# Output projection as seven half-block products per 256 tokens, with row additions on GpSimd and the variance on ScalarE

## What is computed

```python
h    = x * (1 + scale(c)) + shift(c)
proj = h @ w_in + b_in            # q, k, v, z_attn, u_x, g_b, g_c, z_conv, g_A, g_B
y_A  = (dilated_window_attention(q, k, v) * silu(z_attn)) @ w_proj_attn
y_B  = (g_b * conv3(g_c * u_x) * silu(z_conv)) @ w_proj_conv
m    = sigmoid(g_A) * y_A + sigmoid(g_B) * y_B
out  = LayerNorm(alpha * x + gate(c) * (m @ w_out + b_out)) * ln_g + ln_b
```

## Time and profile before

| | |
|---|---|
| median of 3 runs | 1869.77 us (1869.06 to 1870.61) |
| the profiled execution's own time | 1868.47 us |
| its span | 1866.7 us |
| PE / VectorE / ScalarE / GpSimd busy | 99% / 65% / 45% / 10% |
| granted TensorE clock, mean | 0.999 of full |

### The profile page before, as it was taken

How to read it: one execution, slowest core, us unless ns; L and a number is a source line. 1 busy time by engine, 2 the same in 40 slices (tenths; PEclk the granted TensorE clock), 3 DMA queues, 4 the chain that set the end, 5 groups by cost and what they waited for, 6 DMA issues and landing times.

```text
span 1866.7 us, 24546 instructions
## 1 busy us (share of the span) xinstructions
PE 1849.8 (99%) x8879; PEld 1508.0 (81%) x8879; DVE 1214.1 (65%) x2086; ACT 840.7 (45%) x1493; POOL 183.0 (10%) x305
## 2 busy tenths in 40 slices
PE   8999999999999999999999999999999999999998
PEld 7788888888888888878878888888888888888886
DVE  8755744456666666675686766666657576646776
ACT  5644633445545555666674545555454310012221
POOL 0223011100000000111210000000111100000000
PEclk9999999999999999999999999999999999999999
DMA  9866523332322222455853222222354988784442
GB/s 372 296 234 242 200 111 113 98 128 72 111 88 95 86 95 82 153 190 180 296 212 101 94 80 91 82 88 87 113 176 135 287 238 225 219 276 135 147 136 101
DMA packets 156648, 292.38 MB, mean 157 GB/s; under 512 B 35344, under 2 KB 87312, under 8 KB 152816
## 3 DMA queue, kind: packets, MB, share of 16 engines
q1 hardware_dynamic: 131056, 202.87, 33.9%
q0 software_dynamic: 25184, 87.35, 12.7%
q10 hardware_dynamic: 288, 0.59, 0.1%
HBM read 202.37 MB, written 88.38 MB: 156 GB/s over the span
## 4 chain that ended last, share of the span: by engine, by line
PE 95%; DVE 2%; ACT 1%; DMA 1%; issue 1%; ACTq 0%; POOL 0%; DVEq 0%
PE acc L1120 22%; PE acc L1125 21%; PE acc L1128 21%; PE acc L1329 3%; PE acc L1278 3%; PE acc L1282 3%; PE acc L1321 3%; PE acc L1325 3%; PE acc L1274 3%; PE score L1185 2%; PE xb L1218 2%; PE acc L1136 1%; PE xb L1201 1%; PE pt_o L1201 1%; DMA vt_d<-room 1%
## 5 line engine op out<-in xcount | busy, mean ns | idle before, releaser
L1120 PE MATMUL acc<-t_hi,w_hi 128*128 128x512 f32 x1848 | 509.2, 397 | 3.0 <-DVE room L1625 1.8
L1125 PE MATMUL acc<-t_lo,w_hi 128*128 128x512 f32 x1848 | 495.0, 390 | 0.0
L1128 PE MATMUL acc<-t_hi,w_lo 128*128 128x512 f32 x1848 | 494.9, 390 | 0.0
L1125 PEld LDWEIGHTS acc<-t_lo,w_hi 128*128 128x128 f32 x1848 | 346.9, 188 | 74.1
L1128 PEld LDWEIGHTS acc<-t_hi,w_lo 128*128 128x128 f32 x1848 | 346.9, 188 | 73.8
L1120 PEld LDWEIGHTS acc<-t_hi,w_hi 128*128 128x128 f32 x1848 | 337.1, 188 | 82.2 <-issue 13.1
L1625 DVE TENSOR_TENSOR room<-acc,part 128x512 f32<-128x512 f32 x198 | 136.8, 691 | 219.7 <-PE acc L1128 213.9
L1421 ACT ACTIVATE part<-acc,cols 128x512 f32<-128x512 f32 x198 | 136.8, 691 | 209.8 <-PE acc L1128 209.4
L1625 DVE TENSOR_TENSOR room<-room 128x512 f32<-128x512 f32 (+3 forms) x223 | 176.5, 795 | 73.8 <-ACT room L1451 30.7
L1625 DVE TENSOR_TENSOR w_lo<-w_raw,w_hi 128x512 fp32r<-128x512 f32 x272 | 183.7, 687 | 40.8 <-ACT w_hi L1404 39.2
L1404 ACT CAST w_hi<-w_raw 128x512 fp32r<-128x512 f32 x264 | 162.8, 617 | 90.2 <-PE acc L1128 87.6
(11 more groups left out here) (224 smaller groups left out, 2067.8 us busy)
## 6 DMA issues: line engine op xcount, KB each, us to landing
w_raw<-in_w_tiles SPq DMA_DIRECT2D x132, 512.0 KB, 4.5
gate_d<-room POOLq DMA_DIRECT2D x64, 256.0 KB, 3.8
w_raw<-gate_d SPq DMA_DIRECT2D x32, 512.0 KB, 5.6
qk_d<-room POOLq DMA_DIRECT2D x24, 512.0 KB, 5.1
room<-qk_d SPq DMA_DIRECT2D x74, 128.0 KB, 3.6
t_raw<-tr_d SPq DMA_DIRECT2D x8, 1024.0 KB, 7.1
conv_d<-room POOLq DMA_DIRECT2D x16, 512.0 KB, 3.0
mix_d<-w_raw POOLq DMA_DIRECT2D x32, 256.0 KB, 5.6
```

What stands on the lines that cost most here:

```text
L1120: nc.tensor.matmul(to, w_hi[:, s, k], t_hi[:, p, k], start=(first and k == 0), stop=False, skip_group_check=True)
L1125: nc.tensor.matmul(to, w_hi[:, s, k], t_lo[:, p, k], start=False, stop=False, skip_group_check=True)
L1128: mm = nc.tensor.matmul(to, w_lo[:, s, k], t_hi[:, p, k], start=False, stop=(last and k == KH - 1), skip_group_check=True)
```

## The change

- The output projection becomes 8 more groups (`NO`) of the ring's scheme, 256 tokens each. The tiles of m take the part of the ring's weights (`load_m` into `w_raw`, then `combine`, `round_w`, `split_w`), the output weights the part of the stationary token blocks: seven 128x2048 blocks, four of them sums. PE runs `product(n)` for n from `NS` = 476 to `NALL` - 1 = 531.
- The four sums of the weights are made in mid-kernel, in four steps of a 1024 KB load, four subtractions of 128x512 on VectorE (`sum_wq`) and a 1024 KB store to `to_d` from GpSimd's queue.
- The seven weight blocks are loaded (`load_to`), rounded and split one by one as the merge gives their room free: blocks 0 to 3 during the last 8 units, blocks 4, 5 and 6 when all of `mc_done` (32) is reached, that is behind the last matmul of the merge.
- The merge's last 8 units use other buffers (`mg_last`), whose reload waits for the store of the tile three units earlier.
- LayerNorm: ScalarE scales x (`scale_x`), GpSimd adds the bias row (`residual`), VectorE adds the products onto it (`take_y`, four of seven with a running sum), ScalarE squares and sums for the variance and takes the root (`deviation`), VectorE subtracts the mean and multiplies by g (`center`), ScalarE divides (`scale_row`), GpSimd adds b and issues the store (`shift_row`). Only the last tile keeps `bn_stats` and halves.

```diff
+NO = NTT // 2
+NALL = NS + NO * NP
...
+            s = (n - NS) % RING
+            return t[1][:, RING - 1] if s == KH else t[0][:, 1, s].rearrange("p (k n) -> p k n", n=P)
...
+                def load_to(p):
+                    sp.wait_ge(mc_done, M0 + (0, 2, 4, 6, 8, 8, 8)[p])
...
+                        sp.wait_ge(t_hi_done, 3 * NP + T_MORE + p - 3)
+                    sp.dma_start(to_raw(p), src).then_inc(t_in[p % 4], 16)
...
+                    if tt in (2, 3, 4):
+                        wait_m_last()
...
+                load_to(4)
+                load_to(5)
+                load_to(6)
+                sp.wait_ge(gb_ready, 1)
...
+                for to, src in ((g_bc, ln_g), (b_bc, ln_b)):
+                    sp.dma_start(to, src.broadcast_to([P, D])).then_inc(bc_in, 16)
+                for tt in range(2, NX):
+                    load_x(tt)
+                for h in range(2, NO):
+                    load_m(h)
+                    for tt in (2 * h, 2 * h + 1):
+                        if tt >= NX:
+                            load_x(tt)
...
+                def residual(tt):
+                    pool.wait_ge(x_scaled, tt + 1)
+                    nc.gpsimd.tensor_tensor(xs[tt % NX], xs[tt % NX], gb, ALU.add).then_inc(r_ready, 1)
+                def shift_row(tt):
+                    pool.wait_ge(normed, tt + 1)
+                    nc.gpsimd.tensor_tensor(xs[tt % NX], xs[tt % NX], b_bc, ALU.add).then_inc(affine, 1)
+                    pool.wait_ge(affine, tt + 1)
+                    pool.dma_start(out2[tt * P:(tt + 1) * P, :], xs[tt % NX]).then_inc(outs[tt % 4], 16)
...
+                for tt in range(4):
+                    residual(tt)
+                pool.wait_ge(bc_in, 64)
+                for h in range(NO):
+                    shift_row(2 * h)
+                    if h < NO - 1:
+                        shift_row(2 * h + 1)
+                    for tt in (2 * h + 4, 2 * h + 5):
+                        if tt < NTT:
+                            residual(tt)
...
-                for tt in range(NTT):
-                    r = tt % 2
-                    pe.wait_ge(m_hi_done, tt + 1)
...
-                        for k in range(KT):
-                            if tt == 0 and half == 0 and k % 2 == 0:
-                                pe.wait_ge(wo_hi_done, k // 2 + 1)
-                            nc.tensor.matmul(to, m_h[:, k], wo_hi[:, k, w], start=(k == 0), stop=False)
...
+                for n in range(NS, NALL):
+                    product(n)
...
+                    act.wait_ge(nmu_ready, tt + 1)
+                    nc.scalar.activation(squares, xs[tt % NX], ACT.Square, bias=nmu[:, r:r + 1],
+                                         accum_out=ssq[:, r:r + 1]).then_inc(squared, 1)
+                    act.wait_ge(squared, tt + 1)
+                    nc.scalar.activation(std[:, r:r + 1], ssq[:, r:r + 1], ACT.Sqrt, bias=eps[:, 0:1],
+                                         scale=1.0 / D).then_inc(std_ready, 1)
...
+                def scale_x(tt):
+                    act.wait_ge(x_in[tt % 4], 16 * (tt // 4 + 1))
+                    nc.scalar.activation(xs[tt % NX], xs[tt % NX], ACT.Identity, bias=0.0, scale=ALPHA).then_inc(x_scaled, 1)
+                def scale_row(tt):
+                    r = tt % 2
+                    act.wait_ge(centered, tt + 1)
+                    nc.scalar.activation(xs[tt % NX], xs[tt % NX], ACT.Identity, bias=0.0,
+                                         scale=rstd[:, r:r + 1]).then_inc(normed, 1)
...
+                for m in range(NS, NALL + 2):
+                    if m + 4 < NALL:
+                        round_w(m + 4)
+                    if m < NS + 3:
+                        round_to(m - NS + 4)
+                    h, p = (m - NS) // NP, (m - NS) % NP
+                    for tt in {1: (2,), 2: (3,), 5: (4, 5)}.get(m - NS, (2 * h + 4, 2 * h + 5) if p == 5 else ()):
+                        if tt < NTT:
+                            scale_x(tt)
+                    if p == 6:
+                        deviation(2 * h)
+                    if p == 0 and h:
+                        deviation(2 * h - 1)
+                        scale_row(2 * h - 2)
+                    if p == 1 and h and 2 * h - 1 < LAST:
+                        scale_row(2 * h - 1)
...
+                        tt_op(wq[:, to], wq[:, a], wq[:, b], ALU.subtract).then_inc(wq_summed, 1)
...
+                def take_y(n):
+                    g, p = at(n)
+                    tile, half, first, done = ((0, 0, None, p1_out), (1, 1, None, p5_out), (0, 1, None, u2_out),
+                                               (0, 0, p1_out, c11_out), (1, 1, p5_out, c22_out), (0, 1, u2_out, c12_out),
+                                               (1, 0, None, c21_dve))[p]
+                    tt = 2 * (g - NG) + tile
+                    y = xs[tt % NX][:, half * CH:(half + 1) * CH]
+                    dve.wait_ge(prod, n + 1)
+                    if first is None:
+                        dve.wait_ge(r_ready, tt + 1)
+                    else:
+                        dve.wait_ge(first, g - 1)
+                    if p < 3 or tt == LAST:
+                        tt_op(y, bank(g, p), y, ALU.add).then_inc(done, 1)
+                    else:
+                        nc.vector.tensor_tensor_reduce(out=y, in0=bank(g, p), in1=y, scale=1.0, scalar=0.0, op0=ALU.add, op1=ALU.add,
+                                                       accum_out=sums_y[:, tile, half:half + 1]).then_inc(done, 1)
...
+                def center(tt):
+                    r = tt % 2
+                    dve.wait_ge(std_ready, tt + 1)
+                    if tt >= 2:
+                        dve.wait_ge(normed, tt - 1)
+                    own_t.up(nc.vector.reciprocal(rstd[:, r:r + 1], std[:, r:r + 1]))
+                    if tt < 2:
+                        dve.wait_ge(bc_in, 64)
+                    dve.wait_ge(nmu_ready, tt + 1)
+                    own_t.wait()
+                    nc.vector.scalar_tensor_tensor(out=xs[tt % NX], in0=xs[tt % NX], scalar=nmu[:, r:r + 1], in1=g_bc,
+                                                   op0=ALU.add, op1=ALU.mult).then_inc(centered, 1)
...
+                for m in range(NS, NALL + 1):
+                    if m > NS:
+                        take_y(m - 1)
+                    h, p = (m - NS) // NP, (m - NS) % NP
+                    if p == 0 and h:
+                        center(2 * h - 2)
+                    if p == 1 and h:
+                        center(2 * h - 1)
+                    for n, when in enumerate((-4, -3, -2, 0)):
+                        if (m - when) % NP == 0 and NG + (when < 0) <= (m - when) // NP < NG + NO:
+                            combine((m - when) // NP, n)
+                    if m + 3 < NALL:
+                        split_w(m + 3)
+                    if NS < m <= NS + 3:
+                        split_to(m - NS + 3)
+                finish_last()
```

380 lines of the change are left out of this document (199 added, 181 removed).

## The result

The changed kernel takes **1922.97 us** (median of 4 runs, 1921.53 to 1923.59) against 1869.96 us for the kernel before: a ratio of 1.0283, 95% interval 1.0270 to 1.0296. It is slower by 53 us; the forecast was 1890 us, slower by 20.

The account below looks back on a forecast made before the run. PE, busy 99% of the span, was taken as the bound. -21.8 + 9 + 2.5 + 30.5 = +20.2 on 1868.5 gives 1888.7, with 1.3 to the median 1890 us; range for 8 in 10, 1857 to 1901.

Parts of the forecast that it names:

- 1 matmuls: Output stage: 672 matmuls for 768, at 0.2267 us each: -21.8 us.
- 2 mid-kernel: Sixteen VectorE subtractions in four mid-kernel steps are covered: price 0; up to 11 us in all if cover failed.
- 3 start: First group of the output stage: late loads delay product 6 and pauses lower the clock: +9 us, between 4 and 14.
- 4 tail: After the last matmul: one more center, then scaling, GpSimd addition and store, 9.8 us instead of 7.35: +2.5 us.
- 6 steady groups: GpSimd's additions hold VectorE up: 4.8 us per group, 28.8 for six groups, 1.7 for the last: +30.5 us.
- The forecast's chain: Stage start: ScalarE scales x's tile 2 before rounding weight block 6, so product 6 starts late; 7.5 us taken.
- term 6: Output stage: GpSimd's additions, 2.4 us each, shut VectorE out: +30.5 us; the first group waits for its loads anyway.
- term 5: Steady group: VectorE has 16.1 us of work and ScalarE 12.4 in 19.04 us; both fit, no stall.
- exclusion: Output stage: VectorE's instructions with two operands in memory wait while GpSimd adds; 1890 us, chance 0.40.
- Rivals one and two: Output stage: GpSimd does not hold VectorE up, 1859.5 us, chance 0.33; they share the path in turns, 1873 us, 0.15.
- rival three: Output stage: PE's pauses pull the clock down in every group, 1.5 us in each of seven: 1900 us, chance 0.12.

Follow-up runs that it names:

- run 1: The change with GpSimd's two additions per tile replaced by bare semaphore increments (gate*b_out and ln_b left out): 1873.18 us.
- run 5: Against run 4: ScalarE scales x tiles 2 and 3 at product 5 of group 0, SyncE stores the row block before last: 1856.28 us.
- run 4: The change without GpSimd's additions (gate*b_out and ln_b left out) and with ScalarE scaling x tiles later, behind the deviations: 1865.93 us.
- run 10: The change with GpSimd's four additions per group replaced by one-operand multiplications by 1.0 (gate*b_out and ln_b left out): 1887.95 us.
- run 13: The change with all additions kept and only the orders repaired as in run 5 (x scaled later, row block before last stored by SyncE): 1901.49 us.

## Why the prediction was right or wrong

The sum was made against the profiled execution, 1868.47 us; that of the change is 1921.53, 53.1 us more. By the prediction's terms:

| term | forecast | measured |
|---|---|---|
| 1 matmuls | -21.8 | -21.8 (8 x 19.04 for 174.07) |
| 2 mid-kernel | 0 | +0.55 (the stage's begin) |
| 3 start | +9 | +10.1 (29.17 - 19.04) |
| 4 tail | +2.5 | +8.2 (15.52 for 7.35) |
| 6 steady groups | +28.8, last group +1.7 | +55.7, last group +0.2 |

**Matmuls and mid-kernel** held: product 2.72, and the stage begins 0.55 us later than in the profile before. How much of that the four steps of subtractions cost can't be told: the same code begins the stage between 1685.7 and 1688.0 us in the other profiles.

**Start** held in size. The forecast's chain is there when it is alone: run 1 has group 0 at 29.26, and run 5 took 6.6 us off run 4's by letting ScalarE round block 6 before it scales x; 4.2 us stay. In the change itself only part of the 10.1 us is that chain. 4.3 are a stand in front of product 2, where a split is held 5.43 us, and 2.3 the slower clock behind it: additions, of which term 6 had said that the first group waits for its loads anyway. One has hidden the other, so the sum came out by chance.

**Tail** failed at its last link. Its way to GpSimd's store was forecast as 6.9 us and took 7.1 (1904.18 to 1911.32). Behind the store I put 2.9 us, the landing; the span went on for 8.4. In the kernel before GpSimd's last instruction lay far ahead of the end, so its trace could not show that.

**VectorE's load** (term 5) was too high: 14.44 us in run 4, where 16.1 was said, for durations were added that overlap by 0.09 us each. This error went against slower and changed little, since what holds VectorE is not its own work.

**GpSimd's additions** (term 6) are the step that failed: the mechanism, exclusion, is right, and the hand-made schedule that priced it is not. Rivals one and two fell: splits of 2.0 us while GpSimd adds, and 50 us gone without them. The Trainium skill's rule (SBUF — State Buffer, Who interferes with whom), that a VectorE instruction with two SBUF inputs contends with a GpSimd instruction that reads SBUF and the second waits the first out: the additions agree (5.69 us), so do the rows with one accumulator operand (0.68) and the memsets. The one-operand reads of run 10 agree that reading holds, but let VectorE go after 0.9 of 2.8 us, and a split that is already waiting when the second addition begins is passed by it; in both the measurement decides. The price per addition, 2.4 us, was right as well (2.52 on average, 2.35 to 2.45 where it had not to wait for VectorE; the estimate of 2.25 from the same skill's GPSIMD Engine Reference, Performance versus the Vector engine, is 11% below the average). Wrong was the schedule, 4.8 us per group for 9.3:

- The hold itself in front of product 6 was forecast as 3.1 and is 4.0 us (run 13, where product 5 takes 6.7 us on average). The forecast's 1.7 in front of product 4 did not come: the single additions there meet slack.
- **The clock**, rival three with a chance of 0.12, came true on top: behind a stand of TensorE of 3.1 to 4.5 us product 6 takes 4.2 to 5.3 us in 11 of the 12 steady groups of the change and run 13, at a granted clock of 0.50 to 0.64. In run 13 that is 1.9 us per group, where the rival had 1.5. The forecast had a pause of 3.1 in its own schedule and the row with the halved clock beside it, and still kept both apart.
- **The order in ScalarE**, in no case of the prediction, is another 2.9 us per group (28.33 for 25.41), net: the wait in front of product 2, 2.6 us on average, and the slower clock behind it. Term 5 asked whether ScalarE's 12.4 us fit and not what its order waits for. A wait was added there, `scale_x` for a load that SyncE issues only behind the last split; what stands behind it on ScalarE was not written down.

These three make 4.0 + 1.9 + 2.9 = 8.8 of the 9.3 us. The rest is in small pieces. Against the schedule's 4.8 us the holds are 0.8 less, the clock is 1.9 more and ScalarE's order 2.9 more: the largest part of the miss is a wait that stood in no term, and the clock is one that the prediction named and left out of its sum.

## What to carry to other kernels

An engine that shares a path with another is not priced by its busy time but by its longest unbroken stretch against the lead of the ring: two additions in a row cost 25 us more than the same two apart, and cutting them in halves changed nothing. Where a stage has VectorE at 14.4 of 19 us, put the row work there, though it looks dearer: 1862 us, where the additions on GpSimd with the same repairs at start and tail take 1901 (run 13). What TensorE then still waits for is a chain between two take-outs, not VectorE's total. And when work moves into an engine's fixed order, write down for each step what it waits for and what stands behind it, on the queue that issues its loads too.

## What the runs showed of the hardware

- A VectorE instruction with two operands in SBUF waits through a whole run of GpSimd additions: 5.69 us for two of 128x1024 (4.71 us), 5.26 for four of 128x512 (4.97). With one operand in the accumulator it keeps its 0.68 us. It goes the other way too: an addition behind a split of 128x2048 took 4.10 us for 2.4.
- GpSimd's memset (1.82 us for 128x2048) holds no such instruction (0.68 us beside it). Its one-operand multiplication (2.77 us for 128x1024) holds one for its first 0.9 us and lets it go for the rest. An addition of the same size, with two operands, takes 2.35 to 2.45 us when it need not wait, less than the multiplication.
- The span goes on for 7.7 to 7.8 us after GpSimd's last instruction (seven kernels); the last store has landed 4.8 us before the end in the change, and no work is recorded behind it. Where GpSimd finished early the span ended 2.5 us after VectorE's last instruction. So in this kernel the last work should not be GpSimd's; why is not shown.
- VectorE's independent instructions of 128x512 show 0.69 us and follow each other every 0.60.
- After TensorE had stood for 3.8 us its granted clock was 0.63 over the next product (in part at 1.2 GHz); after 1.5 us it was 1.00. In between the length of the stand alone does not tell: after 2.3 us it was 0.61 (run 5, group 0), after 2.5 us 1.00 (the change, group 4), after 3.1 us once 0.64 and once 1.00 (the change, groups 3 and 5).
